# A hybrid GLA and retention decoder step on one core: the decode normalization is moved behind the GLA keys with a buffer per group, and the GLA mixture's rounding copies go to ScalarE

## What is computed

```python
h = _rmsnorm(x, norm_w)
z = jnp.einsum('btd,dc->btc', h, w_in).astype(F32)
gq, gk, gv, gg, glr, rq, rk, rv, rg = _split_cols(z)
...
if chunked:                                       # the prompt
    o_a, s_gla_new = _gla_chunked(q_a, k_a, v_a, la, s_gla)
    o_b, s_ret_new = _ret_chunked(q_b, k_b, v_b, s_ret)
else:                                             # the 8 decode tokens
    o_a, s_gla_new = _gla_recurrent(q_a, k_a, v_a, la, s_gla)
    o_b, s_ret_new = _ret_recurrent(q_b, k_b, v_b, s_ret)
o_a = o_a * lax.rsqrt(jnp.mean(o_a * o_a, axis=-1, keepdims=True) + EPS) * gla_norm_w
o_a = o_a.reshape(B, T, GLA_WIDTH) * jax.nn.silu(gg)
mu = jnp.mean(o_b, axis=-1, keepdims=True)
var = jnp.mean(jnp.square(o_b - mu), axis=-1, keepdims=True)
o_b = ((o_b - mu) * lax.rsqrt(var + GN_EPS)).reshape(B, T, RET_WIDTH)
o_b = (o_b * ret_norm_w + ret_norm_b) * jax.nn.silu(rg)
mixed = jnp.concatenate([o_a, o_b], axis=-1)
y = x + jnp.einsum('btc,cd->btd', mixed, w_out)
```

## Time and profile before

| | |
|---|---|
| median of 3 runs | 1829.59 us (1827.66 to 1830.8) |
| profiled execution | 1829.18 us |
| its span | 1827.4 us |
| TensorE clock granted, mean | 0.991 |
| TensorE busy | 1776.0 us |
| VectorE, GpSimd, ScalarE busy | 918.2, 839.0, 684.0 us |
| HBM traffic over the span | 114 GB/s |

### The profile page before, as it was taken

One profiled execution on the slowest core, in us unless ns is written; L12 is line 12 of the kernel. 1 busy time (PEld: TensorE's weight loads), 2 busy tenths in 40 slices (PEclk: granted clock), 3 DMA queues, 4 the chain that ended last, 5 costly groups with the idle time before them and its releaser, 6 DMA issues.

```text
span 1827.4 us, 26886 instructions
## 1 busy us (share of the span) xinstructions
PE 1776.0 (97%) x10410; PEld 1435.5 (79%) x10410; DVE 918.2 (50%) x2303; ACT 684.0 (37%) x1291; POOL 839.0 (46%) x657
## 2 busy tenths in 40 slices
PE   5999999989999999999999999998999999999996
PEld 3777878878788888888877777887877888888885
DVE  4434534666354462554533436466654555564464
ACT  3433245332353325332443424433234343353323
POOL 2345434564344643454433444555535454454543
PEclk8999999999999999999999999999999999999998
DMA  3322246432342234422442224373243322352232
GB/s 138 118 71 77 87 140 200 140 98 99 121 157 75 81 127 128 140 74 81 141 142 94 70 73 149 116 228 108 80 139 116 139 81 82 127 188 71 91 104 98
DMA packets 98462, 209.63 MB, mean 115 GB/s; under 512 B 12832, under 2 KB 15264, under 8 KB 98336
## 3 DMA queue, kind: packets, MB, share of 16 engines
q10 hardware_dynamic: 73728, 134.25, 22.1%
q1 hardware_dynamic: 24608, 73.67, 12.4%
HBM read 185.99 MB, written 21.89 MB: 114 GB/s over the span
## 4 chain that ended last, share of the span: by engine, by line
PE 91%; DVE 3%; issue 2%; ACT 1%; POOL 1%; DMA 1%; SPq 0%; POOLq 0%; ACTq 0%
PE bank L589 73%; PE bank L756 3%; PE bank L760 2%; PE bank L770 2%; PE bank L735 2%; PE bank L323 2%; PE bank L598 2%; PE bank L793 1%; PE bank L552 1%; PE bank L817 1%; DMA w_stage<-in_w_slots 1%; PE bank L811 1%; POOL w_lo L253 1%; PE bank L718 1%; DVE m_hi L1317 1%
## 5 line engine op out<-in xcount | busy, mean ns | idle before, releaser
L253 POOL TENSOR_TENSOR w_lo<-w_stage,w_hi 128x512 fp32r<-128x512 f32 x252 | 339.3, 1362 | 445.4 <-ACT w_hi L246 445.4
L253 POOL TENSOR_TENSOR w_lo<-ss,w_hi 128x512 fp32r<-128x512 f32 x208 | 273.4, 1325 | 323.7 <-ACT w_hi L246 323.7
L589 PE MATMUL bank<-h_hi,w_hi 128*128 128x512 f32 x1024 | 412.7, 403 | 0.2 <-ACT region L930 0.2
L589 PE MATMUL bank<-h_hi,w_lo 128*128 128x512 f32 x1024 | 400.4, 391 | 0.0
L589 PE MATMUL bank<-h_lo,w_hi 128*128 128x512 f32 x1024 | 400.3, 391 | 0.0
L246 ACT ACTIVATE w_hi<-w_stage 128x512 fp32r<-128x512 f32 x252 | 149.4, 627 | 539.9 <-PE bank L589 367.3
L589 PEld LDWEIGHTS bank<-h_hi,w_hi 128*128 128x128 f32 x1024 | 192.6, 188 | 54.3 <-issue 14.4
L246 ACT ACTIVATE w_hi<-ss 128x512 fp32r<-128x512 f32 x208 | 125.0, 625 | 269.1 <-PE bank L589 178.4
L589 PEld LDWEIGHTS bank<-h_hi,w_lo 128*128 128x128 f32 x1024 | 192.6, 188 | 41.5
L589 PEld LDWEIGHTS bank<-h_lo,w_hi 128*128 128x128 f32 x1024 | 192.9, 188 | 36.9
L589 PE MATMUL bank<-w_hi,h_hi 128*128 128x512 f32 x512 | 205.1, 401 | 9.5 <-DVE region L1380 9.5
(11 more groups left out here) (188 smaller groups left out, 2398.1 us busy)
## 6 DMA issues: line engine op xcount, KB each, us to landing
w_stage<-in_w_slots ACTq DMA_DIRECT2D x252, 256.0 KB, 2.9
ss<-in_w_slots ACTq DMA_DIRECT2D x208, 256.0 KB, 2.9
v_b<-in_w_slots ACTq DMA_DIRECT2D x52, 256.0 KB, 2.9
xn<-in_x_prompt SPq DMA_DIRECT2D x20, 512.0 KB, 4.3
region<-in_x_prompt SPq DMA_DIRECT2D x16, 512.0 KB, 4.0
out_acts<-region SPq DMA_DIRECT2D x16, 512.0 KB, 3.5
xn<-out_acts SPq DMA_DIRECT2D x16, 512.0 KB, 4.8
region<-out_acts SPq DMA_DIRECT2D x16, 512.0 KB, 3.9
```

Source lines behind the costliest of these rows:

```text
L253: pool.tensor_tensor(w_lo[:, r, c], stage(h), w_hi[:, r, c].bitcast(f32), ALU.subtract).then_inc(lo_done, 1)
L589: i = pe.matmul(P[q][:, :], x, y, start=(s == 0 and kk == 0 and c == 0), stop=(s == 3 and kk == 1 and c == 2), skip_group_check=True)
```

## The change

Two parts. The first gives `o_d` a buffer per group, moves `sample_normed(0)` from VectorE's window 16 to the end of its window 17, `sample_affine(0)` from the head of window 18 to its end, and TensorE's `sample_outputs_t(0)` from behind window 17 to behind window 18; ScalarE's copy for group 1 no longer waits for the transposes of group 0. The second takes the rounding copies of the GLA mixture from VectorE to ScalarE, where they stand ahead of `split_hi` in windows 26 and 27, and orders VectorE's work as two products and then two differences.

```diff
-        z = sb("z", [128, 512])
-        z_u, z_v, o_d = z[:, 0:128], z[:, 128:256], z
+        o_d = sb("o_d", [128, 2, 512])
+        z_u, z_v = o_d[:, 0, 0:128], o_d[:, 0, 128:256]
...
                             if w == 17:
+                                sample_outputs(1)
+                            if w == 18:
                                 sample_outputs_t(0)
-                                sample_outputs(1)
...
                             act.wait_ge(so_ps.sem, so_ps.at(l, 1 + w // 18))
-                            act.wait_ge(ot_ps.sem, ot_ps.at(l, 1)) if w == 18 else act.wait_ge(v_out, l * 32 + 32)
-                            nc.scalar.activation(o_d[:, :], (X, ST)[w // 18][:, :], ACT.Copy).then_inc(od_sb.sem, 1)
+                            if w == 12:
+                                act.wait_ge(v_out, l * 32 + 32)
+                            nc.scalar.activation(o_d[:, w // 18, :], (X, ST)[w // 18][:, :], ACT.Copy).then_inc(od_sb.sem, 1)
...
+                        if w in (26, 27):
+                            for t in (2 * (w - 26), 2 * (w - 26) + 1):
+                                act.wait_ge(mix_sb.sem, mix_sb.at(n, 4 + t + 1))
+                                nc.scalar.activation(m_hi[:, 0:4, TOK * t:TOK * t + TOK], tmp[:, t % 2, :].rearrange("p (h n) -> p h n", h=HEADS), ACT.Copy).then_inc(mhi_sb.sem, 1)
                         for h in (2 * (w + AHEAD - 1), 2 * (w + AHEAD - 1) + 1) if w > 0 else ():
                             split_hi(act, n * HALVES + h)
                             load_half(act, n * HALVES + h + 2)
...
-                            if w == 16:
+                            if w == 17:
                                 sample_normed(0)
+                            if w == 18:
+                                sample_affine(0)
...
                             vec.scalar_tensor_tensor(dst, src, parh[:, 0:1], gate, ALU.mult, ALU.mult).then_inc(mix_sb.sem, 1)
-                            tile = slice(TOK * t, TOK * t + TOK)
-                            vec.wait_ge(mix_sb.sem, mix_sb.at(n, 4 + t + 1))
-                            vec.tensor_copy(m_hi[:, 0:4, tile], dst).then_inc(mhi_sb.sem, 1)
-                            vec.wait_ge(mhi_sb.sem, mhi_sb.at(n, 4 + t + 1))
-                            vec.tensor_tensor(m_lo[:, 0:4, tile], dst, m_hi[:, 0:4, tile].bitcast(f32), ALU.subtract).then_inc(mlo_sb.sem, 1)
+
+                    def mixed_rest(t):
+                        dst = tmp[:, t % 2, :].rearrange("p (h n) -> p h n", h=HEADS)
+                        tile = slice(TOK * t, TOK * t + TOK)
+                        vec.wait_ge(mhi_sb.sem, mhi_sb.at(n, 4 + t + 1))
+                        vec.tensor_tensor(m_lo[:, 0:4, tile], dst, m_hi[:, 0:4, tile].bitcast(f32), ALU.subtract).then_inc(mlo_sb.sem, 1)
...
-                        if w == 18 and kind == 1:
-                            sample_affine(0)
...
                         if w in (26, 27):
                             mixed(1, 2 * (w - 26))
                             mixed(1, 2 * (w - 26) + 1)
+                            mixed_rest(2 * (w - 26))
+                            mixed_rest(2 * (w - 26) + 1)
```

More of the change, by code:

```diff
@@ L648, in sample_outputs_t @@
                         for c in range(4):
-                            i = pe.transpose((ATT, X)[g][:, 128 * c:128 * c + 128], o_d[:, 128 * c:128 * c + 128], ident[:, :])
+                            i = pe.transpose((ATT, X)[g][:, 128 * c:128 * c + 128], o_d[:, g, 128 * c:128 * c + 128], ident[:, :])
                         i.then_inc(ot_ps.sem, 1)
@@ L1121, in sample_moments @@
                         for c in range(4):
-                            i = vec.bn_stats(obn[:, c, :], o_d[:, 128 * c:128 * c + 128])
+                            i = vec.bn_stats(obn[:, c, :], o_d[:, g, 128 * c:128 * c + 128])
                         step(i)
@@ L1140, in sample_normed @@
                         for c in range(4):
-                            oc = o_d[:, 128 * c:128 * c + 128]
+                            oc = o_d[:, g, 128 * c:128 * c + 128]
                             if g == 0:
```

## The result

The changed kernel takes 1806.37 us (median of 4 runs, 1806.24 to 1808.45), the kernel before 1828.62 us on the same chip (4 runs, 1827.07 to 1830.8). The ratio is 0.9878, 95% interval 0.9867 to 0.989. The forecast was 1808, range 1804 to 1814.

The account below looks back on a forecast made before the run. TensorE, busy 97%, was taken as the bound, so only its late starts count. 11.3 us (decode normalization) plus 10.0 us (GLA mixture) made 21.3 us off 1829.18, 1807.9, called 1808 for the median; range 1804 to 1814.

Parts of the forecast that it names:

- Part one, 11.3 us forecast: Decode normalization, blocks 1 and 5: 7.8 us of stall plus 3.5 us of clock, between 7.8 and 11.3 us.
- The stretch: Window 16 to window 17, blocks 1 and 5: 3.90 us shorter in each, 7.8 us together.
- 3.5 us were forecast for it: Window 17, blocks 1 and 5: the clock no longer falls behind the stall, 1.36 + 2.14 us.
- the 1.15 us that stay: Window 16, blocks 1 and 5: lateness that remains because VectorE reaches the product late, waiting for ScalarE's L982.
- Part two, 10.0 us forecast: GLA mixture, window 27 of eight blocks: stalls of 6 x 1.28 + 2 x 1.18 us go; bounds 4 to 10.
- the fourth rival: ScalarE in windows 26 and 27: a weight slot comes late and the kernel is slower, 1840 us; chance 0.03.
- The sentence that TensorE has no wait for weights: Argument against a slower kernel from late weight slots: TensorE has no wait for weights in the present trace.
- 0.8 of 1.27 us of a stall: Window 27: if a difference takes 1.66 us after all, some 0.8 of the 1.27 us stall stays.
- the whole 1665 ns for both: VectorE's differences of tiles 2 and 3, window 27: long form 1665 ns each, against the short form's 691 ns.
- The second: Part stays: clock still falls in blocks 1 and 5, 1811.8 us, or differences stay long, 1814; chance 0.15.
- The third: Window 17: another wait replaces L1380's, so only the GLA mixture's gain counts, 1819.6 us; chance 0.04.

Follow-up runs that it names:

- e1_part_one: The kernel before with only the edits to the decode part: 1816.63 us, ratio 0.9935 to the kernel before.
- e2_part_two: The kernel before with only the edits to the GLA mixture: 1818.97 us, ratio 0.995 to the kernel before.
- e3_normed_back: The changed kernel with the normalization of group 0 put back into VectorE's window 16: 1818.65 us, ratio 0.9948 to the kernel before.
- e4_move_only: The kernel before with only the normalization moved from window 16 to 17: 1818.36 us, ratio 0.9949 to the kernel before.
- e11_one_buffer: The changed kernel with one buffer of decode outputs for both groups: 1806.29 us, ratio 0.988 to the kernel before.
- e9_affine_ahead: The changed kernel with ScalarE's affine copy ahead of its second load's staging wait, windows 16 and 17, second block of a layer: 1807.29 us, ratio 0.9884 to before.
- e10_quarter_back: The changed kernel with one of the four normalization operations put back into VectorE's window 16: 1811.45 us, ratio 0.9909 to the kernel before.
- e7_copies_late: The changed kernel with ScalarE's two copies behind the making of w_hi and its two loads, windows 26 and 27: 1807.55 us, ratio 0.9875 to before.
- e5_copies_only: The changed kernel with VectorE's old order, product then difference tile by tile, copies on ScalarE: 1806.28 us, ratio 0.987 to the kernel before.

## Why the prediction was right

**What bounds the kernel.** Right: what came off did so at the two lines of VectorE that TensorE waited for, with the clock behind one of them, and the parts add (`e1_part_one`, `e2_part_two`). One wait was overlooked: a line of ScalarE, L930, holds TensorE up once as well, in block 5, for 0.2 us before and 0.8 after.

**Part one, 11.3 us forecast.** The four moved operations are through at 381.96 and TensorE transposes their result at 387.80, so nothing waits for them. The stretch gives 3.90 us in either block, as worked out (7.1 us of window 16 forecast, 7.07 measured). TensorE starts 0.82 us after the read of unit 3 starts, as before. The clock stays up behind the remaining 0.83 us of wait; 3.5 us were forecast for it. The 24 matmuls of window 17 now take 5.6 us instead of 6.9 and 7.7, which is 3.3 together; the 3.7 of the account also hold some small work that moved with the transposes, and windows 19 and 20 take 0.16 of it back. That the place of the normalization makes the stall and the fall is shown by `e3_normed_back`. What wasn't priced is how part one divides: the later transposes, with the affine step behind them, are worth 1.0 us a block in the windows and 0.85 in the times (`e4_move_only`), the second buffer nothing (`e11_one_buffer`). The prediction said of the buffer that it spares ScalarE a long wait and is no gain of its own. The wait is long, 5.95 us, but covered.

The prediction put the 1.15 us that stay down to ScalarE's L982, which sits behind GpSimd. That is only half of it: `e9_affine_ahead` took this wait away, and the stretch stayed at 7.08 us, since the product then ran beside `w_lo` and took 1.0 us longer.

The Trainium skill (TensorE: Matmul & The Clock Gate, Part 1) describes the fall after a stretch without work and a moment of return that shifts; the trace agrees, and `e10_quarter_back` shows the same for the fall, which came behind one 2.04 us wait and not behind the other.

**Part two, 10.0 us forecast.** 10.2 measured in the windows, in the profile of part two alone as well, and 9.3 in its times. The steps came out within 0.2 us: 1.41 us for two products, 1.29 for two copies, differences of 0.69 throughout (691 to 696 ns over all 32), `w_hi` about 2.4 us later after the slower start of this execution is taken off. In windows 27 and 28 ScalarE nowhere waits for a weight load, so the fourth rival is out. The sentence that TensorE has no wait for weights is true of its direct waits only: ahead of L932 in block 5 stand two waits of ScalarE for loads, in TensorE's window 8, where the change adds nothing (last section).

Where the reasoning was right for too narrow a reason is the place of the copies. The working leaned on `w_lo` starting only after them, and gave 0.8 of 1.27 us of a stall back where it doesn't. `e7_copies_late` shows no stall in that case. The price of a difference beside GpSimd was taken as the whole 1665 ns for both. In `e7_copies_late` only one of the two is long. The first starts when GpSimd's first operation has 0.16 us left, and takes 0.71 us; the second takes 1.77 and ends 0.55 us behind GpSimd's second operation, which fits a wait for that end. Even before the change only tile 2's difference was long in this window; tile 3's took 0.69 us (234.13 to 234.82). What decides is that the copies leave VectorE's chain.

**Rivals.** The second (the clock falls all the same, or long differences) didn't come. For the clock the margin is not known well: it held behind 0.91 us and fell once behind 2.04. The third and fourth found nothing in the trace.

## What to carry to other kernels

Where one engine is the bound and waits at few places, price each place by the whole window against the same window elsewhere, not by the wait figure: here 5.5 us of recorded wait for the differences stood for 10.2 us. Look at what stands ahead of the late operation in its engine's fixed order and ask whether it is wanted there; one moved line gave 9.9 of part one's 11.6 us. Shorten the late engine's chain first (here a copy went to an engine that was idle at that moment), and tune order and place only if the trace still shows a wait.

## What the runs showed of the hardware

**Short stalls and the clock.** In front of window 17 the clock never fell with TensorE waits of 0.83 to 0.91 us (18 cases in nine profiles). It fell with 2.04 us in one of two cases, with 3.27 us in both, and with 4.7 us in all six (the kernel before, `e2_part_two`, `e3_normed_back`). Each fall was to the 1.2 GHz level. With 2.04 us, and with 3.27 us in both blocks, it came 0.2 to 0.8 us after TensorE had started again; with 4.7 us it came during the wait in four cases and 0.3 to 0.4 us after the restart in two. A fall costs 1.3 to 2.4 us: the 24 matmuls of window 17 take 5.6 us in the changed kernel, 6.9 and 7.7 in the kernel before, and at most 8.1, in block 1 of `e2_part_two`.

**The start of a run decides 2 us.** The first large matmul of the run meets the low clock in some executions and not in others. TensorE's timeline of the kernel before, of the changed kernel and of `e5_copies_only`:

```profile
34.86 0.80 PE L589 MATMUL bank<-h_hi,w_hi 128*128 128x512 f32 x1
```

```profile
35.13 0.80 PE L589 MATMUL bank<-h_hi,w_hi 128*128 128x512 f32 x1
```

```profile
33.84 0.50 PE L589 MATMUL bank<-h_hi,w_hi 128*128 128x512 f32 x1
```

From there to window 26 of block 0 it takes 188.3 us in the first, 188.6 in the second and 186.6 in the third (starts at 223.14, 223.70 and 220.42). All 14 profiles fall into these two groups: seven with a first matmul of 0.80 us and 188.3 to 188.8 us to window 26, seven with 0.50 or 0.51 us and 186.6 us. The spread between the runs of one kernel, 2.0 to 4.3 us, is of this size or up to twice as large. A wait of TensorE for one line of ScalarE in block 5 (L932 in the changed kernel) adds to it, with 0.2 to 1.6 us from profile to profile. It has its origin in the weight loads: in the changed kernel ScalarE waits 3.66 and 3.22 us for two loads just before L932. All 14 profiles have this pair of waits. `w_hi` behind the second starts 5.2 to 6.6 us into TensorE's window 8, and TensorE's wait is each time what exceeds 5.1 us.

```profile
1191.41 0.63 ACT L246 ACTIVATE w_hi<-w_stage 128x512 fp32r<-128x512 f32 x1 [3.66 <-DMA w_stage<-in_w_slots]
...
1195.26 0.63 ACT L246 ACTIVATE w_hi<-w_stage 128x512 fp32r<-128x512 f32 x1 [3.22 <-DMA w_stage<-in_w_slots]
...
1195.79 2.04 ACT L932 ACTIVATE region<-bank 128x512 f32<-128x512 f32 x4
...
1196.52 0.47 PE L589 MATMUL bank<-h_hi,w_hi 128*128 128x512 f32 x1 [0.76 <-ACT region L932]
```

Differences of 1 us between variants can't be read from the times; they were read from the windows.
